# One block-diagonal product of two heads, or two products on 128x64 column tiles

## The reference, cut to what matters

```python
def step(state, inp):
    r_t, w_t, k_t, v_t, a_t, b_t = inp
    sa = jnp.einsum('bhvk,bhk->bhv', state, a_t)
    state = state * w_t[:, :, None, :] + sa[..., None] * b_t[:, :, None, :] + v_t[..., None] * k_t[:, :, None, :]
    return state, jnp.einsum('bhvk,bhk->bhv', state, r_t)
```

## Time and profile before

| | |
|---|---|
| two executions | 4013.25 and 4017.34 us, median 4015.3 |
| the profiled execution, first to last instruction (the page gives no other time of it) | 4014.3 us |
| TensorE busy | 3625.6 us (90%) |
| weight loads busy | 2769.2 us (69%) |
| VectorE, ScalarE, GpSimd busy | 1480.2, 1021.5, 778.1 us |
| mean granted TensorE clock | 0.948 |

### The profile page before, as it was taken

How to read it: one execution, slowest core, us unless ns; L and a number is a source line. 1 busy time by engine, 2 the same in 40 slices (tenths; PEclk the granted TensorE clock), 3 DMA queues, 4 the chain that set the end, 5 groups by cost and what they waited for, 6 DMA issues and landing times. The chain is left out here.

```text
span 4014.3 us, 46368 instructions
## 1 busy us (share of the span) xinstructions
PE 3625.6 (90%) x17694; PEld 2769.2 (69%) x17694; DVE 1480.2 (37%) x2586; ACT 1021.5 (25%) x1775; POOL 778.1 (19%) x462
## 2 busy tenths in 40 slices
PE   4999999979999999999999998786988879999996
PEld 3888888735666666666666666665765758888885
DVE  4222222323545445555545444451132142222224
ACT  2111111112333333333333333332122121111111
POOL 2222222001111121112111111112222232122120
PEclk7999999989999999999999999887988979999998
DMA  3111111020000000000000000005210111111111
GB/s 99 53 42 52 52 42 52 17 71 24 26 15 20 20 11 20 20 15 17 23 14 22 18 20 14 1 3 163 71 32 10 48 53 51 43 52 47 47 37 42
DMA packets 205025, 148.43 MB, mean 37 GB/s; under 512 B 8768, under 2 KB 194240, under 8 KB 204352
## 3 DMA queue, kind: packets, MB, share of 16 engines
q1 hardware_dynamic: 204864, 146.21, 11.9%
HBM read 133.60 MB, written 12.58 MB: 36 GB/s over the span
## 5 line engine op out<-in xcount | busy, mean ns | idle before, releaser
L804 PE MATMUL bank<-work,arena 128*128 128x512 f32 x1536 | 769.3, 616 | 8.9 <-DMA arena<-w_in 8.9
L390 PE MATMUL bank<-h_high,w_high 128*128 128x512 f32 x1408 | 555.5, 395 | 22.6 <-POOL h_low L249 14.5
L390 PE MATMUL bank<-h_low,w_high 128*128 128x512 f32 x1408 | 552.7, 393 | 0.0
L390 PE MATMUL bank<-h_high,w_low 128*128 128x512 f32 x1408 | 552.5, 392 | 0.0
L361 POOL TENSOR_TENSOR w_low<-ffn_work,w_high 128x1024 fp32r<-128x1024 f32 x132 | 319.9, 2445 | 1080.2 <-ACT w_high L419 1080.2
L794 PEld LDWEIGHTS bank<-work 128*128 128x128 f32 x3072 | 368.1, 195 | 87.3 <-issue 66.7
L794 PE MATMUL bank<-work 128*128 128x64 f32 (+1 forms) x3072 | 367.1, 277 | 26.8 <-DVE work L1233 25.8
L804 PEld LDWEIGHTS bank<-work,arena 128*128 128x128 f32 x1536 | 262.5, 194 | 167.5 <-issue 158.4
L464 DVE TENSOR_TENSOR ffn_work<-ffn_work,bank 128x512 f32<-128x512 f32 x88 | 60.5, 687 | 814.0 <-ACT ffn_work L427 814.0
L390 PEld LDWEIGHTS bank<-h_high,w_high 128*128 128x128 f32 x1408 | 266.7, 189 | 88.1 <-DVE h_low L249 14.0
L473 DVE SCALAR_TENSOR_TENSOR arena<-bank,arena 128x512 f32<-128x512 f32 x352 | 241.3, 691 | 194.9 <-PE bank L404 194.9
(11 more groups left out here) (246 smaller groups left out, 4990.0 us busy)
## 6 DMA issues: line engine op xcount, KB each, us to landing
arena<-w_in SPq DMA_DIRECT2D x48, 512.0 KB, 3.8
ffn_work<-w_gate SPq DMA_DIRECT2D x44, 512.0 KB, 3.9
ffn_work<-w_up SPq DMA_DIRECT2D x44, 512.0 KB, 3.8
ffn_work<-w_down SPq DMA_DIRECT2D x44, 512.0 KB, 3.7
cross_work<-w_ckv SPq DMA_DIRECT2D x16, 512.0 KB, 4.0
work<-x SPq DMA_DIRECT2D x1, 4096.0 KB, 14.5
x_spill<-arena SPq DMA_DIRECT2D x1, 4096.0 KB, 15.1
m_spill<-work SPq DMA_DIRECT2D x16, 256.0 KB, 2.3
```

What stands on the lines that cost most here:

```text
L390: last = mm(bank[:, 2 * n + b, :], w[wp][:, 2 * f + b, kt], h[hp][:, kt, tok], start=kt + wp + hp == 0, stop=kt == KT - 1 and wp == 1)
L804: last = mm(bank[:, unit % 2, :], panel[j % 3][:, kt], hT[:, kt, n * HALF:(n + 1) * HALF], start=kt == 0, stop=kt == KT - 1)
```

## The change

`per_chunk` makes two products in place of each one. Each takes all 128 rows, but only the 64 stationary columns of one head, and writes only that head's 64 partitions of PSUM. The moving operand is the same for both. The operands, the zeros in them, the order of the calls, the semaphores (one increment on the last product of a call) and all other engines' programs stay as they are. From this line on, line numbers rise by two.

```diff
                     def per_chunk(out, lhs, rhs, chunks=range(NC)):
                         for i, n in enumerate(chunks):
-                            last = mm(out[:, i, :], lhs[:, n, :], rhs(n), start=True, stop=True)
+                            for e in range(2):
+                                last = mm(hs(out, e)[:, i, :], lhs[:, n, e * CH:(e + 1) * CH], rhs(n), start=True,
+                                          stop=True)
                         return last
```

## The result

The changed kernel took 3917.8 us, the median of 3915.28 and 3920.25, against 4015.3: a ratio of 0.9758, 95% interval 0.973 to 0.9786. The forecast was 4064 us, no change on the slow side; the time is rival B's, 3907, to 11 us. It lies outside the forecast's own range, 4014 to 4130, and inside the whole one, 3895 to 4145, only because that took in B.

What follows compares the result with a forecast made beforehand. The prediction took TensorE to bound the kernel in the mixer. Its terms summed as 0 + 27 + 22 = +49 us on 4014.3, giving 4064 us; own range 4014 to 4130, whole range 3895 to 4145.

Steps and rivals of the forecast that it cites:

- rival B: In per_chunk, both heads' loads and multiplies run fully side by side: -157 + 28 + 22 = -107 us, 3907; chance 0.28.
- Part (1): More records in per_chunk: a load of 64 columns takes 56 ns, perhaps 58, against 112 for a full one.
- Term (2): The 1408 per_chunk products with 64 moving columns: four loads of 56 ns take 223 ns, as now: 0 us.
- term (3): The 256 per_chunk products with 128 moving columns: 328 ns each against 223, +27 us; ends 0 and +54 us.
- Part (4): Going between 128 and 64 columns, 224 changes at 0.1 us: 22 us; upper figure 0.33 us each, 74 us.
- Part (5): Other engines: programs unchanged, VectorE and GpSimd wait as now, nothing added; that cover is gone only in rival B.
- C: Rival for per_chunk: the two tiles never overlap, +54 + 22 = +76 us, 4090; chance 0.16.
- D: Rival for per_chunk: load no longer hidden, +417 us, or no longer shorter, +371 us; 4385 to 4453; chance 0.18.

Runs made afterwards that it cites:

- experiment 1: The changed kernel with per_chunk's two loops swapped, all of a call's products of head 0, then all of head 1: 3991.5 us, 0.9938 of the kernel before.
- experiment 3: The changed kernel with only the products of 64 moving columns divided: 3914.2 us, 0.9742; with only those of 128 divided: 4014.3 us, 0.9991.
- experiment 4: The changed kernel with all the mixer's projection products divided too, 854 changes between 128 and 64 columns for 224: 3995.7 us, 0.9944 of the kernel before.
- experiment 6: The kernel of experiment 5 with the scan's products and fills divided too: 3827.4 us, 0.9533; the same with the scan's fills whole: 3912.2 us, 0.9735.
- experiment 5: The changed kernel with projection products divided only in the fills after the triangles and in the levels, 160 changes for 224: 3921.7 us, 0.9758.
- experiment 2: The changed kernel with the heads alternating every two chunks in place of every one: 3926.1 us, 0.9772 of the kernel before.

## Why the prediction was wrong

**The bound was right.** TensorE was the bound in the mixer, and what left it left the time: mixer -97 us, span -101, with no wait of the earlier trace rows longer by more than 2.1 us.

**Part (1) was right.** A load of 64 columns has half the pitch of one of 128, 58 against 112 ns (experiment 1), the upper of the two values there (56 or 58).

**The failed step is the order in parts (2) and (3):** "a load beginning with the multiply ahead of it", and with it that the forecast lets the second head's load wait for the first head's second multiply. The changed kernel's loads have a mean pitch of 28 ns, each tile keeps its own 58, and a record of the other tile passes three that wait for their own tile (experiment 1). I read a limit of one load ahead from rows with one tile. The runs fit a limit of each tile by itself; the rows of the kernel before could not tell that from a limit of the whole queue. Term (2) was 0 and measured (117 - 223) x 1408 = -149 us; term (3) was +27 and measured about 0 (experiment 3).

That is what the Trainium skill ("TensorEngine Tiling (Array Packing)", Key Properties) states: different tiles load weights and multiply in parallel. The trace agrees: 117 ns for four pairs of records that take 4 x 58 on one tile. The other page's rule, that a load overlaps a running multiply only with another row group ("TensorE: Matmul & The Clock Gate", What overlaps and what doesn't), does not hold here: all products take all 128 rows, and loads of both tiles run beside multiplies of both.

**Part (4) was somewhat low.** 0.1 us a change, measured 0.12 (experiment 4) and 0.18 (experiment 6, where the changes stand in the densest stretch), and nothing where a wait follows (experiments 3 and 5). At 0.14, an estimate between the first two, the 224 are 31 us where I had 22. The Trainium skill ("TensorEngine Tiling (Array Packing)", Key Properties) says that a mode change drains TensorE. That a change costs something agrees; that it is a drain no run shows. My upper figure of 0.33 us, the array empty and the load open, is about twice what was measured.

**Part (5) holds for the forecast only, and rival B's second half came true.** B had put VectorE's chain at 0.44 us a level, 28 us in all. In the level above, the growth's loads end at 1002.40 and z begins at 1002.60; the z of the second group waits again, for the add that starts at 1002.79 and ends at 1003.20. The level bears it out: its 16 products should save 16 x 0.106 = 1.70 us and save 0.90, and of the missing 0.80 two changes are 0.28, which leaves 0.52 for the waits and the restarts behind them, 33 us over 64 levels. Together: -149 + 31 + 33 = -85. One sign that I gave for B did not come: VectorE's first add of a level still waits for TensorE (2.08 us; 146.0 in all for 157.0 before), only the second follows at once.

The timelines give the same by place: 64 levels 0.90 us shorter each (those with two fills too), 16 triangles 0.75, 16 first z's 0.58 and 16 last growths 0.31, which is all that the wait before the scan leaves of their 0.64. That is 84 us. The mixer stretch is 97 us shorter. Added up one by one, the 16 ways from the triangles to the scan are 91 us shorter, 644.4 to 553.7: thirteen by 5.1 to 5.3 us, and the ninth and the last two by 6.8, 6.7 and 9.9. In these three the kernel before ran in part at a low clock (mean granted clock 0.96, 0.92 and 0.85, now 1.00, 0.90 and 0.90, and 1.00 before and now in an undisturbed one, the fifth), where an undivided level costs more: 6.72 us from growth to transposes in the last one, for 3.52. The last half pass, before and changed (the clock is the figure ahead of the last two):

```profile
2640.30:2684.40 44.10, 39.64 (x254) 34.91 (x254) 20.79 (x42) 10.54 (x20) 11.74 (x10) 0.85 0.00 1
```

```profile
2553.22:2587.47 34.25, 28.94 (x463) 21.63 (x463) 20.10 (x43) 10.43 (x20) 11.73 (x10) 0.90 0.01 2
```

That is 7 of the 13 us between 84 and 97, and no term of the prediction had it. The other 6 lie between half passes, in stretches that the change leaves alone: 1054.8 us before, 1049.2 now, and 1049.3 to 1053.9 in experiments 1, 2, 3 and 5, which leave them alone too. What moves them stays open. So some of the 97 is no term of B's, and that the time came within 11 us of B's 3907 is in part luck: B had -157, +28 and +22, which the estimates above make -149, +33 and +31, and the difference of 22 us is half made up by what neither had.

**The chances.** B had 0.28, the forecast 0.38. What spoke for B was the half-empty multiply slot, and that is what was filled; what spoke against was the reading above. C (no overlap of tiles) and D (load no longer hidden or no longer shorter) are refuted by the 28 and 58 ns.

## What to carry to other kernels

Compare the pitch of a product with its multiply alone. If the pitch does not fall with fewer moving columns, the weight load sets it, and dividing the stationary columns over two tiles about halves it (223 to 117 ns here, in fp32), even at all rows and with twice the instructions; if load and multiply are as long, it gains nothing. Keep a divided stretch unbroken: divide its neighbours too, even those that gain nothing by it, because each way in or out costs 0.12 to 0.18 us, unless it stands ahead of a wait anyway. And a limit read from one resource (one tile) says nothing of two.

## What the runs showed of the hardware that I had not expected

- In fp32 neither the loads nor the multiplies of the two tiles slow each other: four of each in 117 ns, the heads' starts 7 ns apart, where one tile needs 4 x 58.
- A record can pass three waiting records of the other tile, multiplies too: 32 records take 1.15 us in alternating order, 1.20 in runs of four a tile and 1.54 in runs of eight.
- A change between 128 and 64 stationary columns costs 0.12 to 0.18 us in a dense stretch.
- A product of 512 moving columns costs the same whole and divided (20 records in 4.46 us, as 10 before).
